# Reordering the opening of a two-layer decoder step: chunk loads, turnings, and two blocks modulated by VectorE

## The chip, the core and the metric

The kernel runs on one core of a Trainium2 chip as one program with an instruction list for each engine: TensorE (PE), VectorE (DVE), ScalarE (ACT), GpSimd (POOL) and SyncE (SP, which here issues most DMAs). The engines meet only at semaphores. The metric is device time in microseconds, lower is better.

## The reference, cut to what matters

Two layers are computed for a prompt of 512 tokens and for 8 decoding sequences of 8 tokens, with a model width of 1024, all in float32. Each layer is modulated RMS norm, one input projection, a mixer (layer 0: gated linear recurrence, layer 1: dilated attention), a gate, an output projection and a gated residual. The change concerns only what layer 0 does before its first projection:

```
ada = silu(c) @ w_ada + b_ada             # c: 1 prompt row, 8 sequence rows; w_ada: 1024 x 3072
shift, scale, gate = split(ada, 3)
h = rmsnorm(x, norm_w) * (1 + scale[:, None]) + shift[:, None]
proj = h @ w_in                           # the columns of head 0 come first
```

## The kernel before, in words

Activations lie with features on partitions, as 8 blocks (k = 0 to 7) of 128 features by 576 columns: 512 prompt tokens and 64 sequence tokens. A float32 product is made of three passes over rounded parts. Each weight piece of 128 x 1024 numbers (512 KB) is split into `w_hi` (ScalarE, `split_hi`, L349) and `w_lo` (VectorE, `split_lo`, L357), and h likewise into `h_hi` and `h_lo`. Head 0's first two tickets, the projections q and f, take weight pieces ("w", 0, 0) and ("w", 0, 1), called here the first and the second weight.

**Opening.** SyncE issues in this order: the identity, x in two halves, chunk 0 of the adaLN weight (four transfers of 512 KB), the first weight, chunk 2, the second weight, chunks 1 and 3, and then the stream of further weights, with a parking of x in DRAM behind the third. A chunk is 512 columns: 0 and 1 are the shift of blocks 0 to 3 and 4 to 7, and 2 and 3 are the scale of the same blocks. The order within each engine is written out by hand:

- TensorE (`first_pe`) turns the row-wise x into blocks (L645, L646, eight times), sums the squares of the blocks over the features by products with ones (`first_norm_pe`, L632, five sums), multiplies the chunks by silu(c) (`first_ada`, L441, 16 instructions per chunk, in the order 0, 2, 1, 3), turns the results to features on partitions (`turn_ada`, L455), runs products of ones that feed nothing (L668), and runs the first two tickets block by block (`first_tickets`, L688, 12 products per block). Chunk 1's products stand behind block 0's and chunk 3's behind block 1's, and then both turnings.
- ScalarE (`first_act`) squares each block (L703), makes the inverse root (Ln and Exp, L705 and L706), splits the first weight ahead of the square of block 6 and the second one behind the root, and then for each block modulates the prompt's columns (L714) and rounds them into `h_hi` (L717). Behind block 3 it copies the products of chunks 1 and 3 out of PSUM (L710).
- VectorE (`first_dve`) copies the turned x to SBUF (L748, L749), scales by the inverse root (`scale_x`, L725; the sequences L763), copies the products of chunks 0 and 2 (L449), adds the bias and makes the amplitudes of four blocks at a time (`amplitudes`, L495, L508, and L742 and L743 for the sequences' columns), and makes the low parts of h (`low`, L729 and L730).
- GpSimd adds pairs of squares (L2606), and once x is parked adds two halves of the identity (L2611).

Blocks 4 to 7 can be modulated only when `amplitudes(1)` is done, which needs chunks 1 and 3 multiplied, copied and turned. Behind the eighth block's products comes step 0 of a loop over the heads, in which ScalarE, VectorE and TensorE work on head 0's tickets and on the next weights.

Of the kernel before, what the change touches and what calls it, by code (L numbers as in the profile page):

```python
# [128 lines left out]
def program(nc, I, O):  # L129
    with ExitStack() as ctx:  # L130
# [59 lines left out]
        at_done, half_out = sem("at_done"), sem("half_out")  # L190
# [444 lines left out]
        def first_pe(pe):  # L635

            pe.wait_ge(s_x[0], 32)
            for k in range(KD):
# [16 lines left out]
                if k == 5:  # L655
                    pe.wait_ge(c_sb, 1)
                    pe.wait_ge(par_done, 1)
                    first_ada(0)
# [3 lines left out]
            pe.wait_ge(s_fold, 16)  # L662
            pe.wait_ge(x_sb, KD)
            first_ada(1)
            turn_ada(adr0[:, 0], 0, ada_t0[:, 0:4])
# [3 lines left out]
            for k in range(KD):  # L669
                first_tickets(pe, k)  # L670
                if k == 0:
                    first_ada(2)
                if k == 1:
# [18 lines left out]

        def first_act(act, chain):
# [3 lines left out]
            for k in range(KD):  # L697
                if k == 6:
                    split_hi(("w", 0, 0))
# [9 lines left out]
            split_hi(("w", 0, 1))  # L709
            copy = lambda out, src: act.activation(out, src, ACT.Copy)  # L710
            for k in range(KD):
                act.wait_ge(n_xr, k + 1)
                act.wait_ge(amp_done, k // 4 + 1)
                chain(act.activation(oz[:, k, 0:TP], oz[:, k, 0:TP], ACT.Identity, scale=amp[:, k, 0:1],  # L714
                                     bias=ada[:, 0, k, 0:1]))
                act.wait_ge(n_hs, k // 4 + 1)
                act.activation(h_hi[:, k, 0:T], oz[:, k, :], ACT.Copy).then_inc(n_hx, 1)  # L717
                if k == 3:
                    first_ada_rows(act, 2, copy)
                    first_ada_rows(act, 3, copy)  # L720

        def first_dve(dve, chain):
# [22 lines left out]
            for k in range(KD):  # L745
# [4 lines left out]
                if k == 6:  # L750
                    split_lo(("w", 0, 0))
                if k == 7:
                    first_ada_rows(dve, 0, dve.tensor_copy)
                if k == 4:
                    dve.wait_ge(par_t, 1)
                    dve.tensor_copy(params[:], X[:, 2, 0:NPAR]).then_inc(par_done, 1)
                    dve.wait_ge(par_done, 1)
            chain(dve.tensor_tensor(lb[:, 0], lbr[:, 0], lbr[:, 1], ALU.max))
            chain(dve.tensor_tensor(lbr, lbr, lb[:, 0].unsqueeze(1).to_broadcast([P, 2, AH]), ALU.subtract))
            dve.tensor_copy(lb[:], lbr).then_inc(lb_in, 1)  # L760
            dve.wait_ge(x_sb, KD)
            dve.wait_ge(n_r, 1)
            chain(dve.tensor_tensor(oz[:, 0:KD, TP:T], xT[:, :, TP:T],  # L763
                                    rn[:, TP:T].unsqueeze(1).to_broadcast([P, KD, TS]), ALU.mult))
            first_ada_rows(dve, 1, dve.tensor_copy)
            scale_x(0)
            scale_x(1)
            amplitudes(0)
            scale_x(2)
            low(0)  # L770
            split_lo(("w", 0, 1))
            low(1)
            scale_x(3)
            low(2)
            scale_x(4)
            scale_x(5)
# [9 lines left out]
            for k in range(4, KD):  # L786
                low(k)
# [1993 lines left out]
```

## Time and profile before

| | us |
|---|---|
| median of 3 runs | 1109.14 (1108.93 to 1109.42) |
| the profiled execution | 1108.2 |
| its span | 1106.6 |
| TensorE busy in the span | 1083.3 |
| VectorE busy | 638.6 |
| ScalarE busy | 508.2 |

The profiled execution's own time is 1.6 us above its span. TensorE's granted clock is 0.999 of full speed over the span. The first 52 us are the opening. The timelines give each instruction's start from the span's beginning and its duration; neighbouring matmul rows overlap, since matmuls are pipelined, so the pace is read from start to start.

### The profile page before, as it was taken

To read this page: it belongs to the slowest core of one execution; us is meant where nothing else is said; L and a number is where in the kernel's file an instruction comes from. 1 tells how busy PE (TensorE), PEld (TensorE's weight loads), DVE (VectorE), ACT (ScalarE), POOL (GpSimd) and SP (SyncE) were. 2 spreads that over 40 slices of the span, in tenths; PEclk is the share of its full clock that TensorE was granted. 3 is DMA by queue.
4 is the path that set the end of the run, shared out by engine and by line. 5 is a ranking of instruction groups with operands and counts; after the bars stand their busy time and mean duration, and the time that the engine had idled before them with its cause. 6 is when DMAs were issued, how large, how long until landed. Compare 5 with 4: busy or idle time off the path is not lost.

```text
span 1106.6 us, 26211 instructions
## 1 busy us (share of the span) xinstructions
PE 1083.3 (98%) x11121; PEld 1034.7 (94%) x11121; DVE 638.6 (58%) x1282; ACT 508.2 (46%) x1041; POOL 151.3 (14%) x156
## 2 busy tenths in 40 slices
PE   8999999999999999999999999999999999999998
PEld 6799999999999998988998999999999999998997
DVE  4776767767676858773537534652464346337332
ACT  4653444444454545642225544552554356356122
POOL 1000010101000000000000720450054015300000
PEclk9999999999999999999999999999999999999999
DMA  9873545454545452219235365236522753273441
GB/s 321 289 209 96 152 131 152 134 150 131 152 131 153 125 154 79 82 60 297 77 87 171 92 163 140 81 88 149 155 62 80 159 134 86 55 160 102 138 118 44
DMA packets 232218, 147.73 MB, mean 133 GB/s; under 512 B 7875, under 2 KB 226205, under 8 KB 231590
## 3 DMA queue, kind: packets, MB, share of 16 engines
q1 hardware_dynamic: 217456, 134.17, 42.7%
q10 hardware_dynamic: 14646, 11.89, 3.2%
q8 instruction: 88, 1.44, 0.6%
q14 instruction: 28, 0.23, 0.1%
HBM read 124.00 MB, written 22.02 MB: 132 GB/s over the span
## 4 chain that ended last, share of the span: by engine, by line
PE 88%; DVE 4%; ACT 3%; DMA 2%; issue 1%; SPq 1%; ACTq 0%; DVEq 0%
PE PJ L384 27%; PE PJ L1716 18%; PE PJ L1422 14%; PE PJ L405 8%; PE X L1843 1%; PE X L1280 1%; PE X L1221 1%; PE X L1400 1%; PE X L1870 1%; PE PJ L688 1%; PE PJ L1744 1%; PE PJ L431 1%; PE X L1402 1%; DMA pre<-in_ada_w_dram 1%; PE X L1808 1%
## 5 line engine op out<-in xcount | busy, mean ns | idle before, releaser
L357 DVE TENSOR_TENSOR w_lo<-raw,w_hi 128x1024 fp32r<-128x1024 f32 (+1 forms) x128 | 157.6, 1243 | 164.7 <-ACT w_hi L349 163.7
L349 ACT ACTIVATE w_hi<-raw 128x1024 fp32r<-128x1024 f32 (+1 forms) x128 | 129.3, 1025 | 161.4 <-PE PJ L1716 69.3
L1716 PE MATMUL PJ<-w_hi,h_hi 128*128 128x256 f32 x600 | 167.3, 287 | 0.9 <-DVE w_lo L357 0.7
L1716 PE MATMUL PJ<-w_lo,h_hi 128*128 128x256 f32 x600 | 164.6, 283 | 0.0
L384 PE MATMUL PJ<-h_hi,w_hi 128*128 128x288 f32 (+1 forms) x736 | 160.7, 300 | 0.6 <-ACT v_ L944 0.6
L384 PE MATMUL PJ<-h_hi,w_lo 128*128 128x288 f32 (+1 forms) x736 | 157.6, 296 | 0.0
L384 PE MATMUL PJ<-h_lo,w_hi 128*128 128x288 f32 (+1 forms) x736 | 157.4, 295 | 0.0
L1716 PE MATMUL PJ<-w_hi,h_lo 128*128 128x256 f32 x480 | 135.8, 283 | 0.0
L384 PEld LDWEIGHTS PJ<-h_hi,w_hi 128*128 128x128 f32 x736 | 118.1, 189 | 4.6 <-issue 3.1
L384 PEld LDWEIGHTS PJ<-h_hi,w_lo 128*128 128x128 f32 x736 | 118.9, 189 | 0.0
L384 PEld LDWEIGHTS PJ<-h_lo,w_hi 128*128 128x128 f32 x736 | 118.8, 189 | 0.0
L1716 PEld LDWEIGHTS PJ<-w_hi,h_hi 128*128 128x128 f32 x600 | 115.0, 192 | 1.7 <-DVE w_lo L357 0.9
L1716 PEld LDWEIGHTS PJ<-w_lo,h_hi 128*128 128x128 f32 x600 | 115.1, 192 | 0.0
L1422 PE MATMUL PJ<-oz_low,w_hi 128*128 128x256 f32 x448 | 96.1, 296 | 0.0
L1716 PEld LDWEIGHTS PJ<-w_hi,h_lo 128*128 128x128 f32 x480 | 92.1, 192 | 0.0
L405 PE MATMUL PJ<-w_hi,h_hi 128*128 128x256 f32 x320 | 91.1, 292 | 0.8 <-DVE q_ L1067 0.8
L405 PE MATMUL PJ<-w_lo,h_hi 128*128 128x256 f32 x320 | 88.1, 283 | 0.0
L1422 PEld LDWEIGHTS PJ<-oz_low,w_hi 128*128 128x128 f32 x448 | 75.6, 190 | 0.0
L405 PE MATMUL PJ<-w_hi,h_lo 128*128 128x256 f32 x256 | 72.4, 283 | 0.0
L898 ACT ACTIVATE dd<-dd 128x576 f32<-128x576 f32 (+1 forms) x64 | 41.4, 657 | 62.7 <-DVE dd L1042 53.2
L405 PEld LDWEIGHTS PJ<-w_hi,h_hi 128*128 128x128 f32 x320 | 61.2, 191 | 3.3 <-issue 1.6
L1189 DVE SCALAR_TENSOR_TENSOR xT<-PJ,ada,xT 128x128 f32<-128x128 f32 (+1 forms) x40 | 17.8, 499 | 75.5 <-PE PJ L1422 75.5
(347 smaller groups left out, 2145.4 us busy)
## 6 DMA issues: line engine op xcount, KB each, us to landing
raw<-in_a_w_in_dram SPq DMA_DIRECT2D x48, 512.0 KB, 4.9
raw<-in_b_w_in_dram SPq DMA_DIRECT2D x64, 256.0 KB, 3.9
raw<-in_ada_w_dram SPq DMA_DIRECT2D x28, 512.0 KB, 3.9
kvc<-in_cache_kv_w_dram SPq DMA_DIRECT2D x24, 512.0 KB, 5.7
pre<-in_ada_w_dram SPq DMA_DIRECT2D x16, 512.0 KB, 9.9
s<-in_state_hgrn_dram SPq DMA_DIRECT2D x8, 1024.0 KB, 8.2
out_hgrn_sample_dram<-s ACTq DMA_DIRECT2D x8, 1024.0 KB, 5.1
raw<-in_a_w_out_dram SPq DMA_DIRECT2D x16, 512.0 KB, 5.1
```

The lines of the kernel that those rows point to most:

```text
L349: act.activation(w_hi[:, i % SPLITS, 0:size], raw[:, n % RAWS, 0:size], ACT.Copy).then_inc(hi_done, 1)
L357: dve.tensor_tensor(w_lo[:, i % SPLITS, 0:size], raw[:, n % RAWS, 0:size], w_hi[:, i % SPLITS, 0:size].bitcast(F32), ALU.subtract).then_in ...
L384: last = nc.tensor.matmul(PJ[:, 2 * s + e, 0:n1 - n0], a[:, k, :], b[:, k, n0:n1], start=(k == 0 and i == 0), stop=(k == KD - 1 and i == 2))
L405: last = nc.tensor.matmul(out_of(tile), a, b[:, k % 4, :], start=(k == 0 and i == 0), stop=(k == KD - 1 and i == len(passes) - 1))
L431: last = nc.tensor.matmul(PJ[q:q + 32, bank, n % 4 * P:n % 4 * P + P], scT[:, k, :], w[:, k, :], start=(k < 4), stop=(k >= 4))
L688: last = pe.matmul(PJ[:, 2 * t + e, 0:HT], a[:, k, :], b[:, k, e * HT:(e + 1) * HT], start=(k == 0 and i == 0), stop=(k == KD - 1 and i == 2))
L898: act.activation(dd[:, x % 2, 0:n], dd[:, x % 2, 0:n], ACT.Exp).then_inc(exp_done, 1)
L1189: dve.scalar_tensor_tensor(out=x, in0=y, scalar=gate, in1=x, op0=ALU.mult, op1=ALU.add)
L1221: last = pe.matmul(gram_at(i)[BL * q:BL * q + BL, n], left[:, t:t + BL], right[:, t:t + BL], start=True, stop=True)
L1280: last = pe.matmul(X[:, c // 2, c % 2 * ADV:(c % 2 + 1) * ADV], kr[:, c], v_[:, g % 2, c], start=True, stop=True)
L1422: last = pe.matmul(PJ[:, 2 * (t % 2) + e, 0:z - x], a[:, n % nk, :], b[:, x:z], start=(n == 0 and i == 0), stop=(n == 2 * nk - 1 and i == 2))
L1716: last = pe.matmul(PJ[:, tile // 2, tile % 2 * 256:tile % 2 * 256 + 256], a, b[:, k, :], start=(first and k == 0 and i == 0), stop=(kk == ...
```

## The change

- SyncE: chunk 2 is issued ahead of the first weight instead of behind it.
- TensorE: the products of chunk 0 move from ahead of the turning of block 6 to behind the turning of block 7 and the second norm sum. Chunk 0 is turned on its own ahead of chunk 2's products. Five products of ones stand between these and chunk 2's turning. Chunk 1's products move from behind block 0's to behind block 1's, chunk 3's with the two turnings from behind block 1's to behind block 2's.
- ScalarE: the first weight's high part moves from ahead of the square of block 6 to behind the inverse root, the second's from there to behind block 0's rounding. Blocks 5 and 7 are no longer modulated here, only rounded, behind a wait for VectorE (`n_mod`).
- VectorE: the first weight's low part moves from between the copies of x to ahead of the first amplitudes. The copy of chunk 2 stands behind the scaling of block 0. Blocks 4 to 7 are scaled ahead of the second amplitudes. Blocks 5 and 7 are modulated here (a multiply and an add with scalars per partition), ahead of and behind the low part of block 4.

```diff
--- before.py
+++ after.py
@@ -187,7 +187,7 @@
         q_sig, z_sig, k_done, g_done, b_done, eb_done, dl_done, qe_done = (
             sem(x) for x in "q_sig z_sig k_done g_done b_done eb_done dl_done qe_done".split())
         sum_done, vs_done = sem("sum_done"), sem("vs_done")
-        at_done, half_out = sem("at_done"), sem("half_out")
+        at_done, half_out, n_mod = sem("at_done"), sem("half_out"), sem("n_mod")
         sub_done, exp_done, lv_done = sem("sub_done"), sem("exp_done"), sem("lv_done")
         gram_ready, gram_read = sem("gram_ready"), sem("gram_read")
         kt_ready, kr_done, kz_done = sem("kt_ready"), sem("kr_done"), sem("kz_done")
@@ -652,25 +652,26 @@
                     first_norm_pe(0)
                 if k == 6:
                     first_norm_pe(1)
-                if k == 5:
-                    pe.wait_ge(c_sb, 1)
-                    pe.wait_ge(par_done, 1)
-                    first_ada(0)
+            pe.wait_ge(c_sb, 1)
+            pe.wait_ge(par_done, 1)
+            first_ada(0)
             first_norm_pe(2)
             first_norm_pe(3)
             first_norm_pe(4)
             pe.wait_ge(s_fold, 16)
+            turn_ada(adr0[:, 0], 0, ada_t0[:, 0:4])
             pe.wait_ge(x_sb, KD)
             first_ada(1)
-            turn_ada(adr0[:, 0], 0, ada_t0[:, 0:4])
+            for _ in range(5):
+                pe.matmul(X[:, 2, 0:P], ones[:], ones[:], start=True, stop=True)
             turn_ada(adr0[:, 2], 1, ada_t0[:, 8:12])
             for _ in range(12):
                 pe.matmul(X[:, 2, 0:P], ones[:], ones[:], start=True, stop=True)
             for k in range(KD):
                 first_tickets(pe, k)
-                if k == 0:
+                if k == 1:
                     first_ada(2)
-                if k == 1:
+                if k == 2:
                     pe.wait_ge(n_r, 1)
                     first_ada(3)
                     turn_ada(adr0[:, 1], 2, ada_t0[:, 4:8])
@@ -690,13 +691,13 @@
                 if k == KD - 1:
                     last.then_inc(pj_ready, 1)
 
+        MADE_BY_DVE = (5, 7)
+
         def first_act(act, chain):
 
             act.wait_ge(ones_done, 2)
             logs_and_exps()
             for k in range(KD):
-                if k == 6:
-                    split_hi(("w", 0, 0))
                 act.wait_ge(x_sb, k + 1)
                 if k >= 4:
                     act.wait_ge(n_ms, (k - 2) // 2)
@@ -706,15 +707,20 @@
             act.activation(rn[:], rn[:], ACT.Exp, scale=-0.5).then_inc(n_r, 1)
             act.wait_ge(lb_in, 1)
             act.activation(lb[:], lb[:], ACT.Exp).then_inc(lb_exp, 1)
-            split_hi(("w", 0, 1))
+            split_hi(("w", 0, 0))
             copy = lambda out, src: act.activation(out, src, ACT.Copy)
             for k in range(KD):
-                act.wait_ge(n_xr, k + 1)
-                act.wait_ge(amp_done, k // 4 + 1)
-                chain(act.activation(oz[:, k, 0:TP], oz[:, k, 0:TP], ACT.Identity, scale=amp[:, k, 0:1],
-                                     bias=ada[:, 0, k, 0:1]))
+                if k in MADE_BY_DVE:
+                    act.wait_ge(n_mod, MADE_BY_DVE.index(k) + 1)
+                else:
+                    act.wait_ge(n_xr, k + 1)
+                    act.wait_ge(amp_done, k // 4 + 1)
+                    chain(act.activation(oz[:, k, 0:TP], oz[:, k, 0:TP], ACT.Identity, scale=amp[:, k, 0:1],
+                                         bias=ada[:, 0, k, 0:1]))
                 act.wait_ge(n_hs, k // 4 + 1)
                 act.activation(h_hi[:, k, 0:T], oz[:, k, :], ACT.Copy).then_inc(n_hx, 1)
+                if k == 0:
+                    split_hi(("w", 0, 1))
                 if k == 3:
                     first_ada_rows(act, 2, copy)
                     first_ada_rows(act, 3, copy)
@@ -747,43 +753,47 @@
                 rows, seqs = x_turned(k)
                 dve.tensor_copy(xT[:, k, 0:TP], rows)
                 dve.tensor_copy(xT[:, k, TP:T], seqs).then_inc(x_sb, 1)
-                if k == 6:
-                    split_lo(("w", 0, 0))
-                if k == 7:
-                    first_ada_rows(dve, 0, dve.tensor_copy)
                 if k == 4:
                     dve.wait_ge(par_t, 1)
                     dve.tensor_copy(params[:], X[:, 2, 0:NPAR]).then_inc(par_done, 1)
                     dve.wait_ge(par_done, 1)
+            first_ada_rows(dve, 0, dve.tensor_copy)
             chain(dve.tensor_tensor(lb[:, 0], lbr[:, 0], lbr[:, 1], ALU.max))
             chain(dve.tensor_tensor(lbr, lbr, lb[:, 0].unsqueeze(1).to_broadcast([P, 2, AH]), ALU.subtract))
             dve.tensor_copy(lb[:], lbr).then_inc(lb_in, 1)
+            def modulate(k):
+                dve.wait_ge(n_xr, k + 1)
+                dve.tensor_scalar(oz[:, k, 0:TP], oz[:, k, 0:TP], amp[:, k, 0:1], ada[:, 0, k, 0:1],
+                                  ALU.mult, ALU.add).then_inc(n_mod, 1)
+
             dve.wait_ge(x_sb, KD)
             dve.wait_ge(n_r, 1)
             chain(dve.tensor_tensor(oz[:, 0:KD, TP:T], xT[:, :, TP:T],
                                     rn[:, TP:T].unsqueeze(1).to_broadcast([P, KD, TS]), ALU.mult))
+            scale_x(0)
             first_ada_rows(dve, 1, dve.tensor_copy)
-            scale_x(0)
             scale_x(1)
+            split_lo(("w", 0, 0))
             amplitudes(0)
             scale_x(2)
             low(0)
             split_lo(("w", 0, 1))
+            scale_x(3)
             low(1)
-            scale_x(3)
             low(2)
-            scale_x(4)
-            scale_x(5)
             low(3)
+            for k in range(4, KD):
+                scale_x(k)
             dve.wait_ge(lb_exp, 1)
             chain(dve.tensor_tensor(lbr[:, 0], lb[:, 0], lb[:, 1], ALU.add))
             chain(dve.reciprocal(lbr[:, 1], lbr[:, 0]))
             chain(dve.tensor_tensor(lb[:, 0], lb[:, 0], lbr[:, 1], ALU.mult))
             chain(dve.tensor_scalar(lb[:, 1], lb[:, 0], -1.0, 1.0, ALU.mult, ALU.add))
             amplitudes(1)
-            scale_x(6)
-            scale_x(7)
-            for k in range(4, KD):
+            modulate(MADE_BY_DVE[0])
+            low(4)
+            modulate(MADE_BY_DVE[1])
+            for k in range(5, KD):
                 low(k)
 
         ctx.enter_context(nc.allow_non_contiguous_dma("weights by feature block"))
@@ -2536,9 +2546,8 @@
                                  cols(adaw[0], 2 * q, 2, c * 512, 512)).then_inc(pre_in[c], 16)
 
             first_ada_in(0)
+            first_ada_in(2)
             for n, (key, src, nk, width, freed) in enumerate(stream):
-                if n == 1:
-                    first_ada_in(2)
                 if n == 2:
                     first_ada_in(1)
                     first_ada_in(3)
```

## Rows read from the trace of the kernel before

**Rows 1.** The page's first part: TensorE's busy time, share of the span, instructions.
```profile
PE 1083.3 (98%) x11121; PEld 1034.7 (94%) x11121; DVE 638.6 (58%) x1282; ACT 508.2 (46%) x1041; POOL 151.3 (14%) x156
```

**Rows 2.** The chain of waits, 14 to 69 us: start, duration, engine, tile and line.
```profile
14.67 10.27 DMA pre<-in_ada_w_dram
...
33.31 1.06 PE PJ L688 x6
...
36.22 1.77 PE PJ L688 x12
...
39.85 1.88 PE X L455 x16
...
41.73 3.29 PE PJ L688 x24
...
45.39 5.83 PE PJ L688 x42
...
68.44 0.92 ACT v_ L944
```

**Rows 3.** TensorE's timeline in the opening: start, duration, instruction, [idle before it, releaser].
```profile
0.99 5.48 PE L2726 MATMUL X<-ones 128*128 128x128 f32 x24 [0.99 <-POOL eps L2601]
...
15.32 0.27 PE L646 MATMUL PJ<-ident,oz 64*128 64x64 f32 x1
...
17.09 1.92 PE L441 MATMUL X<-pre,scT 128*32 128x512 f32 x16 [1.49 <-DMA pre<-in_ada_w_dram]
...
21.54 3.18 PE L632 MATMUL X<-nsq,ones 128*128 128x288 f32 x12
...
28.79 2.92 PE L668 MATMUL X<-ones 128*128 128x128 f32 x24
...
34.29 1.92 PE L441 MATMUL X<-pre,scT 128*32 128x512 f32 x16
...
37.92 1.92 PE L441 MATMUL X<-pre,scT 128*32 128x512 f32 x16
...
39.78 1.95 PE L455 MATMUL X<-fold,oz 128*128 128x9 f32 x16
```

**Rows 4.** The windows view, 17 to 28.8 us: busy times, clock, DMA share, GB/s.
```profile
17.00:28.80 11.80, 11.35 (x75) 6.93 (x75) 6.07 (x13) 5.25 (x8) 1.95 (x2) 1.00 1.08 366
```

**Rows 5.** VectorE's timeline in the opening.
```profile
20.58 1.21 DVE L357 TENSOR_TENSOR w_lo<-raw,w_hi 128x1024 fp32r<-128x1024 f32 x1
...
26.31 0.69 DVE L763 TENSOR_TENSOR oz<-xT,rn 128x512 f32<-128x512 f32 x1 [2.70 <-ACT rn L706]
...
28.97 0.30 DVE L495 TENSOR_TENSOR ada<-X,params 128x36 f32<-128x36 f32 x2
...
31.37 0.75 DVE L730 TENSOR_TENSOR h_lo<-oz,h_hi 128x576 fp32r<-128x576 f32 x1
...
41.84 0.30 DVE L495 TENSOR_TENSOR ada<-X,params 128x36 f32<-128x36 f32 x2 [3.64 <-PE X L455]
...
44.54 0.75 DVE L730 TENSOR_TENSOR h_lo<-oz,h_hi 128x576 fp32r<-128x576 f32 x1
```

**Rows 6.** ScalarE's timeline in the opening.
```profile
24.75 0.74 ACT L705 ACTIVATE rn<-X,eps 128x576 f32<-128x576 f32 x1 [1.51 <-PE X L632]
...
26.73 1.06 ACT L349 ACTIVATE w_hi<-raw 128x1024 fp32r<-128x1024 f32 x1 [0.42 <-DMA raw<-in_a_w_in_dram]
...
43.38 0.69 ACT L717 ACTIVATE h_hi<-oz 128x576 fp32r<-128x576 f32 x1
```

**Rows 7.** The timelines of GpSimd and VectorE, 44 to 63 us.
```profile
44.56 0.90 POOL L2611 TENSOR_TENSOR twice<-ident 128x64 f32<-128x64 f32 x1 [19.26 <-DMA xpark<-xT]
...
61.41 1.51 POOL L860 TENSOR_TENSOR qe<-qe,q_ 128x512 f32<-128x512 f32 x1
...
61.69 1.55 DVE L1042 TENSOR_TENSOR dd<-b_ 128x288 f32<-128x288 f32 x1
```

**Rows 8.** One line's instructions in the whole run: minimum, median, maximum ns.
```profile
L1093 DVE TENSOR_SCALAR k_<-fg x8: 459/460/460, 56.2 to 426.2; 128x576 f32<-128x576 f32 x8
```

## The prediction

> **What bounds the kernel now.** I read the page's first part, then the chain of waits, then each engine's timeline over the first 52 us. TensorE is busy for 98% of the span [rows 1], and the chain runs almost wholly over its products, so what the opening gains or loses reaches the end unless a later idle stretch takes it up. The reader should see in the chain [rows 2] that four things tie the opening in turn: the landing of an adaLN chunk at 24.94 (14.67 + 10.27); VectorE and ScalarE making the first block of h and the second weight's low part until 33.31; TensorE's own mixture of chunk products, turnings and first-ticket products until 45.02 (41.73 + 3.29); then the last four blocks from 45.39 on, whose first ticket is complete at about 51.2. Step 0 comes directly behind them. A chain of ScalarE and VectorE starts there from that ticket and is what TensorE waits for near 69.4, behind ScalarE's copy of v (68.44 + 0.92 [rows 2]). It starts from the same event, so it moves with it and absorbs nothing. I find nothing between there and the end that is tied to an absolute time, so the shift of the last four blocks' end is the shift of the kernel.
>
> **The head: turnings, squares and the norm's sum.** Before, TensorE ends its turning of x block 5 at 15.59 (15.32 + 0.27) and stands 1.49 us for chunk 0, because that chunk's products are written ahead of the turning of blocks 6 and 7 [rows 3]. In the new order those two blocks and the second sum go first and the chunk products (1.9 us) behind them; nothing that they read is late. So the same work, from 17.09 to 24.72 (21.54 + 3.18 [rows 3]), starts 1.45 us sooner and ends at 23.3. The squares of blocks 6 and 7 end by about 20.1, ahead of the last sum, and don't hold it. ScalarE's Ln and Exp, begun at 24.75 [rows 6], begin at 23.35, and VectorE scales from 24.9, not 26.31 [rows 5]: 1.4 us gained at this point.
>
> **Second chunk ahead of the first weight.** One transfer of 512 KB no longer stands ahead of chunk 2. At 366 GB/s [rows 4] that is 1.4 us: chunk 2 lands at 23.5. The bytes ahead of what follows are the same: the first weight lands at 24.9, where chunk 2 did, and the second at 26.7 (26.73 [rows 6]) as before. SyncE's later waits are on the splits of these weights (its fourth weight goes out only behind the parking of x, past 31 us, and the first weight's split is done by 28.7) and, after the fifth weight, on the fourth chunk product, which holds three small constant loads that nobody needs until 50 us. Bounds: chunk 2 between 23.5 and 24.94, the weight between 24.9 and 26.7.
>
> **Chunk 0 turned alone.** Two chunks are turned in 1.88 us [rows 2], one in 0.95. TensorE turns chunk 0 from 23.3 to 24.3, chunk 2's products run to 26.2, five fillers of 0.24 us (2.92 / 12 [rows 3]) to 27.4, and chunk 2's turning ends at 28.3, not 28.8. VectorE: the sequences 24.9 to 25.7, block 0 to 26.3, chunk 2's copy to 26.9, block 1 to 27.5. Now comes what the old order did at 20.58 in a gap: the first weight's low part, 1.21 us [rows 5], because ScalarE can make its high part only at 25.1 to 26.2, when the weight is there. It ends at 28.65. So the first amplitudes start at 28.65, not 28.97. Of 1.4 us gained 0.3 is left; 1.15 is VectorE's own work moved onto the path. With chunk 2 at 24.94 the start would be 29.6, 0.6 later than before; with the weight at 26.7 it would be 29.1.
>
> **First blocks.** Block 0's low part ends 3.15 us behind the amplitudes, as before (31.37 + 0.75 - 28.97 [rows 5]): 31.8. The second weight's high part (1.06 [rows 6]) now lies on ScalarE behind block 0, to 31.85, its low part to 33.1, and the second ticket's block-0 products start at 33.15 instead of 33.31, 4.5 us behind the amplitudes instead of 4.34 (0.16 lost), and end at 34.13. Block 1 leaves ScalarE at 33.3, and VectorE, behind the weight's low part and scaled block 3, is done with it at 34.55: block 1's products start at 34.65, with 0.52 us of standing where the old order had a chunk's products.
>
> **The last two chunks, one block further back.** Before: block 0, chunk 1 (34.29), block 1, chunk 3 (37.92), turnings (39.78 [rows 3]), blocks 2 and 3. New: block 0, block 1, chunk 1, block 2, chunk 3, turnings, block 3. A block takes 1.77 [rows 2] and a chunk 1.86 (39.78 - 37.92). From 34.65: block 1 to 36.42, chunk 1 to 38.28, block 2 to 40.05, chunk 3 to 41.91. The turnings start 2.13 us later than before. The second amplitudes follow by 2.06 (41.84 [rows 5] - 39.78): 43.97. Block 3's products run to about 45.4, and TensorE stands. The chunks' data give no reason to wait: chunk 3 lies behind 4.72 MB from chunk 2's landing at 24.94, 12.9 us at 366 GB/s, so it lands by 37.8; the old order used it as it came, the new one lets it lie.
>
> **Second half.** Before, 3.55 us pass from the second amplitudes to block 4's products (45.39 - 41.84), VectorE scaling blocks 6 and 7 ahead of low part 4, which ends at 45.29 (44.54 + 0.75 [rows 5]). Now all scaling is done earlier. ScalarE's copy of block 4 ends 2.23 us behind the amplitudes' start (43.38 + 0.69 - 41.84 [rows 5, 6]) and the low part takes 0.9 more: with handing over, 3.25. VectorE modulates block 5 in the 0.9 us in which it waits for that copy. The trace has no such instruction here. Nearest are VectorE's tensor_scalar of 576 columns, 0.46 us [rows 8], which I take as it is the same kind, and at the far end ScalarE's 0.69 for a block [rows 6]; an added instruction can't cost less than nothing. Both fit. Block 7's lies behind low part 4 and delays low part 5 by as much, but block 5 is due only 1.67 us after block 4 (12 of 42 products that take 5.83 [rows 2]) and its low part takes 0.9, so up to 0.7 is free; without that cover it would be 0.5. What ScalarE saves is worth nothing, since the last four blocks already ran at TensorE's pace. Block 4 starts at 43.97 + 3.25 = 47.2.
>
> **Sum.** -0.32 (first amplitudes) + 0.16 (second weight) + 0.52 (stand before block 1) + 1.77 (one more block ahead of the turnings) - 0.30 (quicker second half) = +1.83; 47.2 - 45.39 says the same. On the profiled execution's 1108.2 us (span 1106.6 and 1.6 around it) that is 1110.0. The median of the three runs, 1109.14, is 0.94 above that execution, so I forecast 1110.9. It is 0.16% more, inside the 0.2% (2.2 us) that I take as what a measurement of this kernel can tell from no change.
>
> **Rivals.** (a) GpSimd's one small sum lands on the second amplitudes. It waits for the parked x and ran at 44.56 for 0.90 us [rows 7]; the amplitudes' operations now run 43.97 to 45.3, and ScalarE's copy of block 4 waits for the last of them. For it: at 61.41 a GpSimd product of 1.51 us stands beside a VectorE instruction of 288 columns that takes 1.55 [rows 7], three times what the 0.46 for 576 columns lets one expect. Against it: this sum has 64 columns, and most of its 0.90 may be waiting. It decides where the parking lands between 43.9 and 45.3. Price 0.3 to 0.9: 1111.2 to 1111.8. The Trainium skill, "SBUF — State Buffer", section on the two separate sides, states that a VectorE instruction with two SBUF inputs and a GpSimd one that reads SBUF shut each other out for a whole instruction. The 1.55 us agrees.
> (b) TensorE drops to its lower clock in the longer stands (0.5 us at 34.1, 1.8 at 45.4). For it: 24 filler instructions took 5.48 us at the start and 2.92 later [rows 3], so the lower level exists here. Against: behind the stand of 1.49 at 15.6 the products ran at full speed. Price 2.56 on top, +4.4: 1113.5.
> (c) The head's gain is kept: the weight's low part slips in beside a wait. The twelve fillers, which now end near 31.2, then bind block 0 and leave 0.7 to 1.0 of it: +0.9 to +1.1, 1110.1. It changes the size, not the sign.
> (d) Faster: TensorE's work alone binds the opening, the stands before blocks 0 and 4 (0.4 each) go and the start moves 0.8 to 1.6 forward. That is -1.6 to -2.4: 1107.5 to 1106.7. It decides if the turnings start by 40, so that the second half is ready when block 3 ends. The order of the program speaks against that.
> (e) Chunk 2 lands no sooner than 24.94: +0.9 on the forecast, 1111.8.
>
> **How the numbers follow.** The forecast 0.54, (a) 0.14, (b) 0.06, (c) 0.10, (d) 0.10, (e) 0.06. Slower than 1111.36: all of (b) and (e), 0.10 of (a) and 0.14 of the forecast, whose own spread is some 0.5 us up and down: 0.36. Faster than 1106.92: 0.08, most of (d). Same: 0.56. The range reaches from 1108.5, which leaves out (d), to 1112.7, which takes in (a) and (e) together and leaves out (b).
>
> **What would show it.** Right: Ln starts near 23.35; the first weight's low part sits on VectorE between block 1 and the first amplitudes; the last two turnings start near 41.9; TensorE stands 1.5 to 2 us before block 4, which starts near 47.2; ScalarE reads the first ticket near 53.0. Wrong: turnings at 40 or sooner, block 4's products directly behind block 3's, or the shift gone again by 70 us.

## The result, and the profile after

The changed kernel takes 1111.88 us in the median of 22 runs (1109.28 to 1114.94), the kernel before 1109.51 in 22 runs beside it (1107.24 to 1113.09). The ratio is 1.0018, 95% interval [1.001, 1.0026], which is +2.0 us (+1.1 to +2.9) on 1109; the two medians lie 2.4 apart. The forecast was +1.8, or 1110.9 us with a range of 1108.5 to 1112.7.

The profiled execution of the changed kernel took 1110.4 us, 2.2 more than that of the kernel before. Its page begins:

```profile
span 1108.8 us, 26229 instructions
...
PE 1083.7 (98%) x11131; PEld 1035.5 (93%) x11131; DVE 639.6 (58%) x1284; ACT 506.1 (46%) x1039; POOL 150.9 (14%) x156
```

TensorE is busy for the same share as in [rows 1], with 0.4 us more of busy time. Second profiles of the two kernels have 1085.8 and 1083.8 us, so this number says little. The ten instructions more are the five products of ones, each of two passes. The chain of waits through the opening (start, duration, engine, tile and line; `first_tickets` is now line 689, the rounding of h line 721):

```profile
23.02 0.75 ACT rn L706
...
27.19 1.14 DVE w_lo L357
...
28.33 0.22 DVE ada L495 x2
...
30.37 1.05 ACT w_hi L349
...
32.72 1.06 PE PJ L689 x6
...
34.17 1.83 PE PJ L689 x12
...
37.86 1.78 PE PJ L689 x12
...
41.50 1.90 PE X L455 x16
...
45.62 0.68 ACT h_hi L721
...
46.74 5.83 PE PJ L689 x42
```

The reader is to see three things beside [rows 2]. The chain no longer starts from a chunk's landing but runs through the root (Ln at 23.02, 24.75 before) and then through VectorE's low part of the first weight (27.19), which was in a gap before. The second weight's high part on ScalarE (30.37) is on it too. And the two turnings end late, at 43.4, so that block 4's products start at 46.74, 1.35 us later than the 45.39 of before. The chain's piece at 45.62 is not what they wait for: it is the rounding of block 5. Block 4's rounding begins at 45.02, and its low part on VectorE follows at 45.88 and ends at 46.63 (45.88 + 0.75, below); the products need both. The name of ScalarE in the brackets of stands ahead of block 4, here and in the runs, is to be read in the same way.

TensorE's timeline (columns as in [rows 3]):

```profile
15.15 0.27 PE L646 MATMUL PJ<-ident,oz 64*128 64x64 f32 x1
...
17.95 1.92 PE L441 MATMUL X<-pre,scT 128*32 128x512 f32 x16
...
19.80 3.18 PE L632 MATMUL X<-nsq,ones 128*128 128x288 f32 x12
...
25.56 1.38 PE L666 MATMUL X<-ones 128*128 128x128 f32 x10
...
35.94 1.92 PE L441 MATMUL X<-pre,scT 128*32 128x512 f32 x16
...
39.57 1.92 PE L441 MATMUL X<-pre,scT 128*32 128x512 f32 x16
...
41.43 1.95 PE L455 MATMUL X<-fold,oz 128*128 128x9 f32 x16
...
46.74 0.50 PE L689 MATMUL PJ<-h_hi,w_hi 128*128 128x288 f32 x2 [1.67 <-ACT h_hi L721]
```

The stand of 1.49 us for chunk 0 is gone: TensorE goes from 15.42 straight on. The last two chunks start at 35.94 and 39.57, where they had started at 34.29 and 37.92, and a stand of 1.67 us lies ahead of block 4, where 0.38 was. The timelines of VectorE, of ScalarE and of GpSimd, one fence each:

```profile
24.58 0.69 DVE L771 TENSOR_TENSOR oz<-xT,rn 128x512 f32<-128x512 f32 x1 [3.45 <-ACT rn L707]
...
27.11 1.22 DVE L357 TENSOR_TENSOR w_lo<-raw,w_hi 128x1024 fp32r<-128x1024 f32 x1
...
28.25 0.29 DVE L495 TENSOR_TENSOR ada<-X,params 128x36 f32<-128x36 f32 x2
...
43.49 0.30 DVE L495 TENSOR_TENSOR ada<-X,params 128x36 f32<-128x36 f32 x2 [3.75 <-PE X L455]
...
44.85 0.55 DVE L766 TENSOR_SCALAR oz<-oz,amp,ada 128x512 f32<-128x512 f32 x1
...
45.88 0.75 DVE L736 TENSOR_TENSOR h_lo<-oz,h_hi 128x576 fp32r<-128x576 f32 x1
```
```profile
25.08 1.06 ACT L349 ACTIVATE w_hi<-raw 128x1024 fp32r<-128x1024 f32 x1 [0.50 <-DMA raw<-in_a_w_in_dram]
...
45.02 1.26 ACT L721 ACTIVATE h_hi<-oz 128x576 fp32r<-128x576 f32 x2
```
```profile
44.63 0.47 POOL L2620 TENSOR_TENSOR twice<-ident 128x64 f32<-128x64 f32 x1 [21.07 <-DMA xpark<-xT]
```

VectorE begins to scale 1.73 us sooner than in [rows 5], and its first amplitudes come only 0.72 sooner: the low part lies between. ScalarE splits the first weight at 25.08, the moment it is there (forecast 25.1). The modulation of block 5 on VectorE takes 0.55 us and ends before the low part of block 4.

Behind the opening the two traces don't keep their distance. It is 1.34 us at the end of the first ticket, 1.23 at 417 us, and 2.47 at 512 us, from where it stays to within 0.02 until past 1080 us; the spans end 2.2 apart. Two places make that, both near TensorE's stands in the last part of layer 0. The changed kernel:

```profile
473.22 0.19 PE L1231 MATMUL X<-qk 128*32 128x32 f32 x1 [1.35 <-issue]
...
512.22 0.53 PE L1432 MATMUL PJ<-h_hi,w_hi 128*128 128x256 f32 x2 [3.16 <-DVE w_lo L357]
```

and the kernel before:

```profile
471.52 0.71 PE L1227 MATMUL X<-qk 128*32 128x32 f32 x23 [0.73 <-issue]
...
509.75 0.53 PE L1422 MATMUL PJ<-h_hi,w_hi 128*128 128x256 f32 x2 [2.68 <-DVE w_lo L357]
```

The first stand (1.35 us against 0.73) has no releaser in the profile. The second waits, through VectorE, for x to be read back from DRAM.

### The profile page after: what moved, and what is told of

It reads as the page before. It is cut to its first block, busy times and chain, and to the rows that moved or that the text cites. A ratio compares the mean times of both kernels' runs of the same rounds, so it can differ in the third digit from the quotient of the medians.

```text
span 1108.8 us, 26229 instructions
## 1 busy us (share of the span) xinstructions
PE 1083.7 (98%) x11131; PEld 1035.5 (93%) x11131; DVE 639.6 (58%) x1284; ACT 506.1 (46%) x1039; POOL 150.9 (14%) x156
## 4 chain that ended last, share of the span: by engine, by line
PE 89%; DVE 5%; ACT 3%; DMA 2%; issue 1%; POOL 0%; SPq 0%; ACTq 0%; DVEq 0%
PE PJ L384 27%; PE PJ L1726 18%; PE PJ L1432 14%; PE PJ L405 8%; PE X L1853 1%; PE X L1231 1%; PE X L1290 1%; PE X L1410 1%; PE X L1880 1%; PE PJ L1754 1%; PE PJ L431 1%; PE X L1412 1%; PE PJ L689 1%; DMA xT<-xpark 1%; PE X L1818 1%
```

## The experiments

Each is given as its edit, what was expected, and what came out. Times in a trace depend by up to 0.4 us on when x lands, so where it matters I count from the start of Ln. "Block 4" is the start of its products; where no stand precedes them it is the last product's start less 6.19 us. "Opening to x" is the time from the opening's last product to the first product behind the reading back of x.

**The changed kernel again.** No edit.

> The changed kernel once more, nothing edited. In its first profile block 4's products start at 46.74 us (45.39 before, +1.35), and the shift grows to +2.47 by 512 us: 0.6 us at 471 us and 0.5 us in the reading back of x at 497 us. Theory A (only the opening's shift belongs to the change, the rest is how one execution differs from another): block 4 again at 46.7, the stand near 472 us and the reading back (9.4 to 9.9 us) come out differently, ratio to before about 1.0012. Theory B (the later 1.1 us belongs to the change as well): both come out the same as in the first profile, ratio 1.002.

1110.98 us in the median of 12 runs, ratio 1.002 [1.0007, 1.0033]. Block 4 at 46.37, the first stand 1.06 us, opening to x 458.64 us (459.29 in the first profile). So block 4 repeats within the landing of x (Ln 0.35 sooner, block 4 0.37 sooner), and the rest varies from execution to execution but stays above the 458.16 of the kernel before. The ratio is the one of theory B; neither theory is settled by it.

**The chunks back behind blocks 0 and 1.**

```diff
-                if k == 1:
+                if k == 0:
                     first_ada(2)
-                if k == 2:
+                if k == 1:
                     pe.wait_ge(n_r, 1)
                     first_ada(3)
```

> The changed kernel, with only the two last chunks put back behind block 0 and block 1. Theory A (the place of these chunks makes the loss): turnings start at 37.4 to 37.9 + 1.86 = 39.3 to 39.8 us instead of 41.43, block 4's products at 44.7 to 45.1 instead of 46.74, 0.3 to 0.7 sooner than the kernel before: ratio 0.9994 to 0.9997 of before. Rival (the splits moved onto VectorE and ScalarE make the loss): block 4 stays near 46.5.

1108.57 us, ratio 1.0004 [0.9992, 1.0015]. TensorE's timeline:

```profile
33.17 1.92 PE L441 MATMUL X<-pre,scT 128*32 128x512 f32 x16
...
37.52 1.92 PE L441 MATMUL X<-pre,scT 128*32 128x512 f32 x16 [0.66 <-DMA pre<-in_ada_w_dram]
...
39.38 1.95 PE L455 MATMUL X<-fold,oz 128*128 128x9 f32 x16
```

Chunk 3's products now wait 0.66 us for their data, the turnings start at 39.38 and block 4 at 44.71, as theory A had it to a tenth. On the same chip, against the same runs of the kernel before, this takes 2.4 us off the changed kernel's median (1110.98 less 1108.57). The rival falls: with all splits as in the change, the loss of the opening is gone. But the gain over the kernel before, 0.7 us in the opening against that kernel's first profile, does not show in the ratio, which was expected at 0.9994 to 0.9997.

**The chunks moved back alone**, in the kernel before: the same edit the other way round.

> The kernel before, with only the two last chunks put one block further back. Theory A: block 1 follows block 0 without a stand (its parts are ready at 34.06), turnings at 41.55, second amplitudes at 43.6, block 4's products at 47.1 instead of 45.39: +1.7 us, more than the whole change. Rival (the splits make the loss): no more than +0.5.

1110.72 us, ratio 1.0015 [1.0003, 1.0026], on its own as much as most of the change. TensorE's and VectorE's timelines:

```profile
47.41 0.51 PE L688 MATMUL PJ<-h_hi,w_hi 128*128 128x288 f32 x2 [2.10 <-ACT h_hi L717]
```
```profile
43.73 0.29 DVE L495 TENSOR_TENSOR ada<-X,params 128x36 f32<-128x36 f32 x2 [5.25 <-PE X L455]
```

Block 4 comes at 47.41, 2.0 us later than in the kernel before (its Ln at 24.43, 0.3 sooner), a little more than the 1.7 expected. The stand ahead of it, 2.10 us where 0.38 was, is what block 2's products (1.77 us), now ahead of the turnings, no longer cover.

**The first weight ahead of chunk 2 again.**

```diff
-            first_ada_in(2)
             for n, (key, src, nk, width, freed) in enumerate(stream):
+                if n == 1:
+                    first_ada_in(2)
```

> The changed kernel, with only the DMA order undone: the first weight again ahead of chunk 2. As forecast, chunk 2 then lands at 24.9 to 25, its products run 25.0 to 26.9, the first amplitudes start at 29.0 to 29.6 us instead of 28.25, and everything behind shifts by the same 0.8 to 1.3 us, block 4's products to 47.5 to 48.0. Rival (the landing of chunk 2 is hidden behind VectorE's work): the first amplitudes at 28.3 to 28.5, nothing behind moves.

1112.88 us, ratio 1.0033 [1.002, 1.0046], the loss larger than expected. TensorE's timeline and the windows view (columns as in [rows 4]):

```profile
25.09 2.80 PE L441 MATMUL PJ<-pre,scT 128*32 128x512 f32 x16 [1.71 <-DMA pre<-in_ada_w_dram]
...
27.82 2.13 PE L666 MATMUL X<-ones 128*128 128x128 f32 x10
```
```profile
25.10:29.80 4.70, 4.70 (x27) 2.49 (x28) 2.36 (x4) 0.03 (x1) 0.00 (x0) 0.64 1.05 383
```

Chunk 2 lands 1.4 us later, as expected: its products start at 25.09, not 23.70. But they take 2.80 us for 16 instead of 1.92, and the ten filler instructions 2.13 instead of 1.38. The granted clock of that stretch is 0.64 of full speed, a mixture of the two levels 1.2 and 2.4 GHz, behind a stand of 1.71 us that itself follows the small products of a turning. The first amplitudes start at 30.78 instead of 29.0 to 29.6 and block 4 at 49.26 instead of 47.5 to 48.0. Counted from Ln, block 4 comes 2.9 us later than in the change, and the median is 1.9 us longer on the same chip (1112.88 less 1110.98). So the DMA order in the change is worth its 1.4 us of landing, and in this profile also the clock.

**Blocks 5 and 7 on ScalarE again.**

```diff
-        MADE_BY_DVE = (5, 7)
+        MADE_BY_DVE = ()
@@
-            modulate(MADE_BY_DVE[0])
             low(4)
-            modulate(MADE_BY_DVE[1])
```

> The changed kernel, with blocks 5 and 7 modulated by ScalarE again. Forecast's theory: the last four blocks run at TensorE's pace of 1.6 us and ScalarE needs 1.4 per block, so nothing changes: block 4 at 46.4 to 46.7 us, last product 6.2 us behind. Rival (VectorE's modulation was what let block 4 come 3.25 us behind the second amplitudes, or holds it up): block 4 more than 0.3 us sooner or later against the second amplitudes, or stands between blocks 4 to 7.

1111.52 us, ratio 1.002 [1.0009, 1.0031]. Block 4 starts 3.25 us behind the second amplitudes (46.78 less 43.53), as with VectorE's help (46.74 less 43.49), and the last product follows 6.19 us later in both. In the opening this part of the change neither costs nor brings anything. The times agree with that, compared through the ratios to the kernel before: 1.002 here, 1.0018 in the result.

**Chunk 0's products ahead of the turning of block 6 again.**

```diff
-            pe.wait_ge(c_sb, 1)
-            pe.wait_ge(par_done, 1)
-            first_ada(0)
             first_norm_pe(2)
@@ in the loop over the blocks of x
+                if k == 5:
+                    pe.wait_ge(c_sb, 1)
+                    pe.wait_ge(par_done, 1)
+                    first_ada(0)
```

> The changed kernel, with chunk 0's products put back ahead of the turning of block 6. Theory: TensorE stands about 1.4 us for chunk 0, the root comes 1.4 us later (Ln at 24.3 to 24.5 instead of 23.0), VectorE starts scaling at 25.9 to 26.0, and as the first weight's low part (1.2 us) lies on this path the first amplitudes start at 29.4 to 29.7 instead of 28.25; all behind shifts by 1.1 to 1.4 us, block 4's products to 47.9. Rival (the head's gain is worth nothing because another thing is late): block 4 stays at 46.4 to 46.9.

1112.56 us, ratio 1.0025 [1.001, 1.004]. TensorE's and VectorE's timelines:

```profile
17.03 1.92 PE L441 MATMUL X<-pre,scT 128*32 128x512 f32 x16 [1.52 <-DMA pre<-in_ada_w_dram]
```
```profile
29.92 0.29 DVE L495 TENSOR_TENSOR ada<-X,params 128x36 f32<-128x36 f32 x2
```

The stand for chunk 0 is back (1.52 us), Ln starts at 24.69, the first amplitudes at 29.92 and block 4 at 48.39, 1.65 us later than in the first profile of the change, a little more than the 1.1 to 1.4 expected. So what the head gains (Ln 1.67 us sooner in the change than here) does reach block 4, in full. What the weight's low part takes back does not show here, as it stands at the same place in both.

**Without the twelve products of ones.**

```diff
-            for _ in range(12):
-                pe.matmul(X[:, 2, 0:P], ones[:], ones[:], start=True, stop=True)
             for k in range(KD):
                 first_tickets(pe, k)
```

> The changed kernel, without the twelve products of ones behind the second turning (they feed nothing), so that TensorE stands 3.7 to 3.9 us from 27.6 to 31.4. Theory: it falls to its lower clock; block 0's products, 12 in about 2.3 us with their wait, and what follows run at half speed for some microseconds, as behind the stand of 1.7 us in the run with the first weight first (granted clock 0.64 over 4.7 us there): block 4 0.5 to 3 us later. Rival (the fillers buy nothing): block 4 at 46.4 to 46.7. Beside it: the stand near 471 us is tied to a place in TensorE's program counted in instructions, so with 24 instructions fewer it comes 24 instructions later, among the products of line 1237 instead of ahead of the last one of line 1231. If it is tied to a wait instead, it stays at its instruction.

1113.16 us, ratio 1.0033 [1.0022, 1.0043]. TensorE's timeline, and the windows view over blocks 0 and 1:

```profile
31.15 0.82 PE L687 MATMUL PJ<-h_hi,w_hi 128*128 128x288 f32 x2 [3.70 <-DVE h_lo L734]
...
473.57 0.31 PE L1430 MATMUL PJ<-h_hi,w_lo 128*128 128x320 f32 x1 [1.52 <-issue]
...
477.42 0.47 PE L1235 MATMUL X<-qk 128*32 128x64 f32 x9 [2.02 <-issue]
```
```profile
31.10:36.90 5.80, 5.75 (x24) 5.78 (x24) 5.05 (x10) 4.14 (x6) 0.00 (x0) 0.50 1.08 388
```

The granted clock is 0.50, the lower level throughout, behind a stand of 3.70 us. Counted from Ln, block 4 comes 1.5 us later than in the change (25.25 against 23.72; 0.5 to 3 expected). The stand that the other runs have near 471 us comes at 475.4 (477.42 less 2.02), behind the 23rd of the 32 products of the group that the change reaches one product after its own stand: 24 instructions later, as expected. A second one of 1.52 us stands ahead of it, and opening to x is 460.68 us.

**The kernel before again.** No edit.

> The kernel before, nothing edited, for a second profile. Between the last of the opening's products and the first product behind the reading back of x, 458.16 us passed in its first profile, 459.29, 458.64 and 458.53 in three of the changed one or its near copies, 458.23 in the one with the chunks moved alone. Theory A (only the opening belongs to the change): 458.2 to 459.3 here as well, the stand of TensorE near 471 us anywhere between 0.7 and 1.4. Theory B (the changed kernel also loses 0.4 to 1.1 us there): 458.2 again.

1109.22 us, ratio 0.9995 [0.9982, 1.0007]. The first stand is 1.24 us, 0.5 longer than in its first profile, and the reading back is quicker by 0.4; opening to x is 458.30. The stand's length belongs to the execution, not to the kernel. Theory B fits better.

**Without the five products of ones.**

```diff
-            for _ in range(5):
-                pe.matmul(X[:, 2, 0:P], ones[:], ones[:], start=True, stop=True)
             turn_ada(adr0[:, 2], 1, ada_t0[:, 8:12])
```

> The changed kernel, without the five products of ones between chunk 2's products and its turning (they feed nothing). Theory: the turning still waits for VectorE's copy of chunk 2 (26.6), ends at 27.6 instead of 27.7, and the first amplitudes, held by VectorE's low part of the first weight, start at 28.2 to 28.3 as before: block 4 at 46.4 to 46.8. As TensorE's program has as many instructions as that of the kernel before again, the stand near 471 us returns behind the ninth product of line 1235's group. Theory B of the time behind the opening (the number of instructions makes it longer): from the opening's last product to the first one behind the reading back of x 458.2 to 458.3 us, as in the three profiles of the old order, and the reading back 9.0 to 9.4. Theory A (it comes from the execution, or from something else of the change): 458.4 to 459.5. Rival on the clock: without the five, TensorE stands 0.9 us at 25.6 and falls to its lower clock, as it did in the run with the first weight first.

1110.27 us, ratio 1.0008 [0.9997, 1.0018]. TensorE's timeline:

```profile
46.39 0.50 PE L687 MATMUL PJ<-h_hi,w_hi 128*128 128x288 f32 x2 [1.66 <-ACT h_hi L719]
...
473.06 0.73 PE L1235 MATMUL X<-qk 128*32 128x32 f32 x23 [1.24 <-issue]
...
510.70 0.53 PE L1430 MATMUL PJ<-h_hi,w_hi 128*128 128x256 f32 x2 [2.10 <-DVE w_lo L357]
```

The opening is that of the change, to 0.02 us of its second profile (block 4 at 46.39), and the clock does not fall in the 1.02 us stand at 25.3. But opening to x is 458.10 us, with the stand again behind the ninth product of the group, as in the kernel before. Theory B again, as far as one profile goes: two profiles of the changed kernel differ by 0.65.

**The five products elsewhere.**

```diff
             for k in range(KD):
+                if k == 4:
+                    for _ in range(5):
+                        pe.matmul(X[:, 2, 0:P], ones[:], ones[:], start=True, stop=True)
                 first_tickets(pe, k)
```

> The changed kernel, with its five products of ones moved into TensorE's stand ahead of block 4 (1.66 us, they take 1.2), so that the opening is as in the run without the five (block 4 at 46.4 us) and the number of TensorE's instructions as in the changed kernel. Five profiles with the number of the kernel before have 457.7 to 458.3 us between the opening's last product and the first one behind the reading back of x, seven with ten instructions more 458.45 to 459.5. Theory (their number shifts where TensorE stands later on): 458.45 to 459.5 here, the stand near 471 us one product ahead of line 1235's group again, time 0.3 to 1.2 us above the run without the five. Rival (what the five do where they stand in the change makes the difference): 457.7 to 458.3, and no time above that run.

1111.01 us, ratio 1.0015 [1.0002, 1.0029]. TensorE's timeline:

```profile
44.67 1.27 PE L671 MATMUL X<-ones 128*128 128x128 f32 x10
...
46.50 0.50 PE L690 MATMUL PJ<-h_hi,w_hi 128*128 128x288 f32 x2 [0.56 <-ACT h_hi L722]
...
472.71 0.19 PE L1232 MATMUL X<-qk 128*32 128x32 f32 x1 [1.09 <-issue]
...
511.16 0.53 PE L1433 MATMUL PJ<-h_hi,w_hi 128*128 128x256 f32 x2 [2.59 <-DVE w_lo L357]
```

Block 4 at 46.50, 0.11 later, with Ln 0.11 later as well. The stand near 471 us is back where the change has it, and opening to x is 458.45 us: at the edge of the expected range, but outside the other. The ratio lies between that of the change and that without the five (1.0008, on another chip); the intervals overlap, so the time alone would not tell them apart.

**The first weight's low part behind the first amplitudes.**

```diff
-            split_lo(("w", 0, 0))
             amplitudes(0)
+            split_lo(("w", 0, 0))
+            low(0)
             scale_x(2)
-            low(0)
```

> The changed kernel, with VectorE's low part of the first weight behind the first amplitudes, and low part 0 ahead of scaling block 2. Theory (that low part is what eats the head's gain): the first amplitudes start when chunk 2's turning ends, 27.7 to 27.8 us instead of 28.25, the first products at 31.0 to 31.3 instead of 31.49; behind that block 1's low part waits for the same VectorE work as before, so block 4 comes no more than 0.3 us sooner: 46.4 to 46.7. Rival (the amplitudes wait for something else): they start at 28.2 again.

1111.8 us, ratio 1.002 [1.0008, 1.0032]. VectorE's and TensorE's timelines:

```profile
28.15 0.30 DVE L495 TENSOR_TENSOR ada<-X,params 128x36 f32<-128x36 f32 x2 [0.58 <-PE X L455]
```
```profile
47.41 0.50 PE L689 MATMUL PJ<-h_hi,w_hi 128*128 128x288 f32 x2 [1.76 <-ACT h_hi L721]
```

x landed late in this execution (Ln at 23.40). Counted from Ln, the first amplitudes start 4.75 us on, 0.48 sooner than in the change and now held by the turning, as the theory had it, and the first products 0.24 sooner. But block 4 comes 0.29 us later (24.01 against 23.72), not a little sooner: the second weight's low part and block 1 wait for the same work of VectorE, now in a worse order. So of the 1.0 us that the low part takes back, this place returns 0.48 at the amplitudes and nothing at block 4. In both places tried, the low part is on the path.

**The best version run**: chunks back behind blocks 0 and 1, and no five products.

> The changed kernel with the two last chunks back behind blocks 0 and 1 and without the five products of ones. Theory: the same opening as in the run with the chunks as before (chunk 3's products wait for their data at 37.5, last product at 51.2, 0.4 to 0.7 us sooner than in the kernel before), and if the number of instructions counts, 0.4 us less behind it: ratio to before 0.9992 to 1.0000.

1108.34 us in the median of 12 runs, against 1109.05 of the kernel before on the same chip, ratio 0.9993 [0.9983, 1.0003]. TensorE's timeline:

```profile
37.76 1.92 PE L441 MATMUL X<-pre,scT 128*32 128x512 f32 x16 [0.51 <-DMA pre<-in_ada_w_dram]
...
39.61 1.95 PE L455 MATMUL X<-fold,oz 128*128 128x9 f32 x16
```

Chunk 3's products wait for their data (0.51 us), the last product starts at 51.12, 0.47 sooner than before, opening to x is 457.70. It beats the changed kernel (the two intervals lie apart); that it beats the kernel before is likely, but not shown, as its interval takes in no change. The last four blocks of this order are bound by the landing of chunk 3.

## Why the prediction was right, and where it was not

The time (1111.88, forecast 1110.9), the sign and the main term were right; that the size of the loss came out as well (2.0, forecast 1.8) is in part luck, as shown below. Point by point, in times of the first profile:

| start of | before | forecast | after |
|---|---|---|---|
| Ln | 24.75 | 23.35 | 23.02 |
| first amplitudes | 28.97 | 28.65 | 28.25 |
| block 1's products | 36.15 | 34.65 | 34.17 |
| the two turnings | 39.78 | 41.91 | 41.43 |
| second amplitudes | 41.84 | 43.97 | 43.49 |
| block 4's products | 45.39 | 47.2 | 46.74 |

**The head.** Gained at the first amplitudes: 0.72 us, not 0.32. Of the difference 0.17 is x landing sooner in that execution (first turning at 8.72, 8.89 before); the rest is small sums in the head that I had rounded against it. That the weight's low part eats most of the gain was right: it stands on the chain, and of 1.73 us gained at Ln it leaves 0.72. It took 1.0 us, forecast 1.15, and putting it elsewhere did not bring block 4 forward. The head is where the opening's forecast missed: every later step kept my distances to 0.1 us (34.65 to 41.91 is 7.26, measured 7.26; to block 4 5.29, measured 5.31).

**The order of chunks and blocks.** The term of +1.77 was shown from both sides: undone in the change it brings block 4 from 46.74 to 44.71, done alone in the kernel before it moves it from 45.39 to 47.41, 2.0 us either way as the profiles stand. Counted from Ln, so without what the head shifts, it is 1.35 and 2.3; where it is undone, chunk 3's landing holds the products back. The two stands with it, forecast as 0.16 and 0.52, are 0.13 (4.47 us from the first amplitudes to the second ticket's products, 4.34 before) and 0.40 in the first profile.

**VectorE's modulation** was costed at nothing, gaining and losing; measured 0.55 and 0.54 us (estimate 0.46, far end 0.69), and nothing moves without it. The trace before had a nearer row than the one that I took: line 1090, the same multiply and add with scalars per partition, takes 0.57 us for 576 columns.

**Chunk 2's landing** was right (its products would have waited until 25.09, by the run with the weight first), but the price of its absence was not: rival (e) gave +0.9, and the run took 1.9 us more than the change; its profile also met the mechanism of rival (b), the lower clock.

**Rivals.** (a) The GpSimd sum did fall between the second amplitudes, at 44.63, for 0.47 us; VectorE's operations beside it kept 0.42, 0.43 and 0.55. Its price was nothing, though it was placed rightly. (b) The clock did not fall in the changed kernel's stand of 1.67 us; it did behind 1.71 us in another place. (c) falls by its mechanism, as the weight's low part stands on the chain and the fillers end at 30.5, 1.0 us ahead of block 0's products (31.49); its size was not far off, since 0.72 us of the head's gain was kept and the opening lost 0.8 to 1.35. (d) falls with the table above: the turnings started at 41.43.

**The step that failed** is "I find nothing between there and the end that is tied to an absolute time, so the shift of the last four blocks' end is the shift of the kernel". The opening's shift at block 4 is 1.35 us in the first pair of profiles and 0.8 to 1.2 over the other pairs, not 1.83, and yet the kernel lost 2.0. The rest comes behind the opening. It goes with the ten instructions (five products of two passes) that I had counted only as 1.2 us of cover. Five profiles with the old number of TensorE instructions have 457.70 to 458.30 us from the opening to x (mean 458.10), eight with ten more have 458.45 to 459.51 (mean 458.74), whatever else they change; the five moved to a place where they cost the opening nothing have 0.35 us more than the same opening without them. Most of the 0.64 us of the means lies behind the start of the reading back of x (13.93 against 14.39 us until the first product). What is shown is that in thirteen profiles it goes with the number of instructions, though the two groups lie only 0.15 us apart, and that the first stand sits at a fixed count of them. Why the reading back then takes longer is not shown, and neither is that the number of instructions is the cause. The lower clock is a rival that the times on record speak against: on the chip of the first four runs, the executions with a granted clock of 1.000 have a median of 1109.5 us in the changed kernel (three) and 1107.3 in the kernel before (five), 2.2 apart, and the others 1111.5 and 1109.0, 2.5 apart. So the total was nearly right by luck: one term was 0.5 us too large and one of 0.6 us was missing.

## What to carry to other kernels

A product that waits for its data as it lands should be put where the data lands, not behind work that can follow it: what stands behind the last chunk in program order is the only cover for the chain that the chunk starts. A gain at the head of an engine's queue is worth what is left after the work that the same edit moves into that queue, so add up the queue before the wait. And where a kernel is tuned to tenths of a microsecond, a comparison should keep the number of instructions equal, or change it alone in a run of its own.

## What the runs showed of the hardware

- TensorE's lower clock can come behind a stand of 1.7 us (granted 0.64 over the next 4.7 us, where the stand followed the small products of a turning), and did not come behind stands of 1.67 and 1.49 us elsewhere. Behind 3.70 us it came in full: 0.50 over the next 5.8 us.
- How far executions of one kernel lie apart goes with it. Of the 22 runs of the changed kernel six have a granted clock of 1.000 over the span and a median of 1109.7 us; the other sixteen, 0.994 to 0.998, have 1112.3. In the second profile of the change the clock is 0.84 from 514 to 520 us, behind the stand for x, and 0.86 from 1012 to 1024 us; in the first profiles of both kernels it is 1.00 in both places. From the first product behind the reading back of x to the end of the span, the four profiles without such a fall have 596.6 to 597.1 us, the seven with one 597.9 to 598.1, and the three with both 599.3 to 599.4: about 1.2 us for each fall. The fall behind the stand for x is in seven of the eight profiles with ten more instructions and in one of the five with the old number.
- A stand of TensorE of 0.7 to 1.6 us near 471 us, with no releaser, sits at a fixed count of its instructions: ten products more move it ten products ahead in the program, 24 fewer move it 24 back. With 24 fewer it takes 2.02 us, and a second one of 1.52 us appeared ahead of it.
- The record says more on these stands. The page of the kernel before has a DMA queue of the kind instruction:

```profile
q8 instruction: 88, 1.44, 0.6%
```

Each of its 88 packets has 16384 bytes. In all fourteen profiles this stand (in the run without the twelve products the one of 2.02 us) lies behind the 5781st of TensorE's recorded products. The stand of 1.52 us lies 128 products ahead of it, which is 256 instructions with the weight loads. One such packet starts 2.2 to 2.8 us before each of these stands ends. 88 times 256 is 22528, near TensorE's 22242 products and weight loads (twice 11121 [rows 1]). So an estimate from these numbers is that a packet holds 256 instructions of 64 bytes, and that TensorE stands there for its next instructions. No run tested it.
